# First attention: the join of both sides' weights on GpSimd in place of VectorE, and second copies of turned weights on VectorE in place of ScalarE

## The reference

```python
def block(args):                      # one row block of 128 queries
    i, qb1, qb2 = args
    qpos = i * QB + jnp.arange(QB)
    mask = kpos[None, :] <= qpos[:, None]
    def probs(qb, k):
        s = jnp.einsum('bhqd,bshd->bhqs', qb, k).astype(jnp.float32) * scale
        return jax.nn.softmax(jnp.where(mask, s, -jnp.inf), axis=-1)
    a = probs(qb1, k1) - lam * probs(qb2, k2)
    return jnp.einsum('bhqs,bshe->bhqe', a.astype(v.dtype), v)
```

## Time and profile before

| | |
|---|---|
| three runs | 2420.66, 2422.44, 2423.96 us |
| the profiled execution | 2422.4 us, and its span is 2422.4 us |
| PE busy | 2333.4 us (96% of the span), 12906 matmuls |
| DVE busy | 1497.8 us (62%), 1897 instructions |
| ACT busy | 989.8 us (41%), 1496 instructions |
| POOL busy | 200.9 us (8%), 254 instructions |
| mean granted TensorE clock | 0.996 of full speed |
| the first attention | about 1368 to 1593 us of the span |

### The profile page before, as it was taken

The page is one execution under the profiler, slowest core; times in us unless marked ns, Lnnn a source line. Parts: engine busy times, 40 slices in busy tenths (PEclk is TensorE's granted clock), DMA queues, the critical chain, the costliest instruction groups (busy, mean ns, idle before and its releaser), DMA issues.

```text
span 2422.4 us, 30366 instructions
## 1 busy us (share of the span) xinstructions
PE 2333.4 (96%) x12906; PEld 1249.1 (52%) x12906; DVE 1497.8 (62%) x1897; ACT 989.8 (41%) x1496; POOL 200.9 (8%) x254
## 2 busy tenths in 40 slices
PE   7999999999999999999999977899999999989999
PEld 5445444444444444445544456654444446777765
DVE  6898856644644455588742389865534416989962
ACT  6245344221212121433322488842323216888841
POOL 0001030000000000533301100012000000000000
PEclk9999999999999999999999999999999999999999
DMA  5011000201111102013111010020130200010021
GB/s 184 35 60 45 1 35 36 104 35 70 36 70 35 70 35 70 1 37 116 59 70 35 1 36 1 1 105 35 70 139 29 76 2 1 1 36 1 1 88 53
DMA packets 50487, 116.02 MB, mean 48 GB/s; under 512 B 2418, under 2 KB 8107, under 8 KB 49968
## 3 DMA queue, kind: packets, MB, share of 16 engines
q1 hardware_dynamic: 48616, 105.40, 12.3%
q10 hardware_dynamic: 1736, 8.68, 0.9%
HBM read 101.49 MB, written 12.58 MB: 47 GB/s over the span
## 4 chain that ended last, share of the span: by engine, by line
PE 81%; DVE 10%; ACT 7%; issue 1%; DMA 0%; SPq 0%; DVEq 0%; ACTq 0%
PE PS L72 78%; PE PS L75 4%; ACT RG L81 3%; DVE mx L110 2%; DVE RG L107 2%; DVE R L93 2%; ACT OV L84 2%; DVE R L101 1%; DVE RG L93 1%; DVE RG L101 1%; ACT R L81 1%; DVE oss L110 1%; ACT mx L81 0%; DVE scl L110 0%; DMA R<-in_x 0%
## 5 line engine op out<-in xcount | busy, mean ns | idle before, releaser
L72 PE MATMUL PS<-R,RG 128*128 128x512 f16 (+1 forms) x5472 | 1163.6, 374 | 8.4 <-DVE R L101 4.2
L72 PEld LDWEIGHTS PS<-R,RG 128*128 128x128 f16 (+1 forms) x5472 | 540.4, 103 | 625.8 <-issue 10.5
L72 PE MATMUL PS<-RG,R 128*128 128x512 f16 (+1 forms) x2904 | 631.3, 378 | 2.2 <-DVE R L101 1.7
L72 PEld LDWEIGHTS PS<-RG,R 128*128 128x128 f16 x2904 | 283.4, 98 | 330.5 <-issue 3.0
L81 ACT ACTIVATE R<-PS,scl 128x512 f32<-128x512 f32 (+1 forms) x176 | 116.2, 685 | 646.8 <-PE PS L72 520.8
L101 DVE SCALAR_TENSOR_TENSOR R<-PS,scl,R 128x512 f32<-128x512 f32 (+1 forms) x227 | 161.5, 744 | 184.2 <-PE PS L72 163.5
L101 DVE SCALAR_TENSOR_TENSOR RG<-RG,scl 128x4096 f16<-128x4096 f32 (+2 forms) x52 | 190.6, 3665 | 54.1 <-ACT RG L81 54.1
L107 DVE TENSOR_TENSOR_SCAN RG<-RG 128x127 f32<-128x127 f32 (+7 forms) x128 | 168.4, 1343 | 80.2 <-ACT RG L81 80.0
L72 PE MATMUL PS<-R,OV 128*128 128x64 f32 (+2 forms) x1456 | 195.7, 276 | 5.7 <-DVE R L93 5.4
L110 DVE TENSOR_REDUCE scl<-RG 128x1 f32<-128x4096 f32 (+2 forms) x43 | 155.6, 3619 | 65.3 <-DMA RG<-in_a_w_in 24.7
L81 ACT ACTIVATE RG<-RG,scl 128x4096 f16<-128x4096 f32 (+2 forms) x52 | 158.6, 3050 | 90.2 <-DVE scl L113 90.2
(11 more groups left out here) (128 smaller groups left out, 1522.3 us busy)
## 6 DMA issues: line engine op xcount, KB each, us to landing
RG<-in_w_ff SPq DMA_DIRECT2D x16, 2048.0 KB, 8.2
RG<-in_a_w_in SPq DMA_DIRECT2D x8, 2048.0 KB, 8.6
xspill<-R ACTq DMA_DIRECT2D x2, 4096.0 KB, 16.3
RG<-in_w_kv SPq DMA_DIRECT2D x4, 2048.0 KB, 8.1
RG<-in_b_w_in SPq DMA_DIRECT2D x4, 2048.0 KB, 8.1
RG<-in_w_in SPq DMA_DIRECT2D x3, 2048.0 KB, 8.3
R<-in_x SPq DMA_DIRECT2D x8, 512.0 KB, 8.3
RG<-in_w_out SPq DMA_DIRECT2D x2, 2048.0 KB, 7.9
```

The costliest lines, as they stand in the source:

```text
L72: return self.engine.matmul(*a, **k) if self.engine else Nothing()
```

## The change

VectorE keeps the reciprocal and the ratio and signals `ratio`. GpSimd's new `join(v)` multiplies `e2` by the ratio in place, one `tensor_scalar` a head, and adds all heads of the group to `ea` with one `tensor_tensor`; it signals `joined_a`. The two partition reductions come after groups 30 and 35 of its loop. VectorE's ratio of v waits in addition for `joined_a` of v-2, whose ratio columns it writes over. Part 1 of the copies (`turned_late`) moves from ScalarE to VectorE, behind the ratio of the same iteration; the last one stands between `finish_half` and `finish_low`. The second products wait for `turned_late`.

```diff
--- before.py
+++ after.py
@@ -435,6 +435,9 @@
         def da_scale(u, c, x=0):
 
             return 8 * (u % 4) + c * len(da_groups[u][1]) + x
+
+        def da_ratio(v, j, n):
+            return oss[:, 8 * (v % 2) + 4 * j:8 * (v % 2) + 4 * j + n]
 
         def l_sum(c, i, h, n=1):
             return ls[:, 64 * c + 8 * i + h:64 * c + 8 * i + h + n]
@@ -892,7 +895,7 @@
                         bo = banks.ap(("pva", i, h // 4))
                         for j in range(i + 1):
                             at = width(i) * x + 128 * j
-                            e.wait_ge(*sig("turned_a").at(v, at // 512))
+                            e.wait_ge(*(sig("turned_late").at(v) if at // 512 else sig("turned_a").at(v, 0)))
                             mm = e.matmul(bo[:, 128 * (h % 4):128 * (h % 4) + 128], AT[v % 2][:, at:at + 128],
                                           VV[:, j, 128 * h:128 * h + 128], start=(j == 0), stop=(j == i))
                     mm.then_inc(*full.up("pva", i, hs[-1]))
@@ -1728,6 +1731,17 @@
                 e.wait_ge(*full.at("za", u, sides[-1]))
                 e.tensor_reduce(out, z, AX.X, ALU.max, negate=True).then_inc(*sig("top_a").up(u, sides[-1]))
 
+            def turned_late(v):
+
+                if 0 <= v < N and len(halves(da_width(v))) == 2:
+                    s, at, n = halves(da_width(v))[1]
+                    e.wait_ge(*full.at("ta", v, s))
+                    if v >= 2:
+                        i, hs = da_groups[v - 2]
+                        e.wait_ge(*full.at("pva", i, hs[-1]))
+                    e.tensor_copy(AT[v % 2][:, at:at + n], banks.ap(("ta", v, s))[:, 0:n]).then_inc(
+                        *banks.empty([("ta", v, s)], sig("turned_late"), v))
+
             N = len(da_groups)
             for u in range(N + 4):
                 if u < da_first:
@@ -1738,19 +1752,16 @@
                 if 1 <= u < N + 1:
                     v = u - 1
                     i, hs = da_groups[v]
-                    w, n = width(i), len(hs)
-                    a, a2 = ea(v), e2(v)
-                    ri, ro = oss[:, 8 * (v % 2):8 * (v % 2) + n], oss[:, 8 * (v % 2) + 4:8 * (v % 2) + 4 + n]
+                    n = len(hs)
                     e.wait_ge(*sig("exp").at(v, 1))
-                    e.reciprocal(ri, l_sum(1, i, hs[0], n)).then_inc(*step.up())
+                    if v >= 2:
+                        e.wait_ge(*sig("joined_a").at(v - 2))
+                    e.reciprocal(da_ratio(v, 0, n), l_sum(1, i, hs[0], n)).then_inc(*step.up())
                     e.wait_ge(*step.last())
-                    e.scalar_tensor_tensor(ro, l_sum(0, i, hs[0], n), lamt[:, 5:6], ri, ALU.mult,
-                                           ALU.mult).then_inc(*step.up())
-                    e.wait_ge(*step.last())
-                    for x in range(n):
-                        ax = a[:, w * x:w * x + w]
-                        join = e.scalar_tensor_tensor(ax, a2[:, w * x:w * x + w], ro[:, x:x + 1], ax, ALU.mult, ALU.add)
-                    join.then_inc(*sig("joined_a").up(v))
+                    e.scalar_tensor_tensor(da_ratio(v, 1, n), l_sum(0, i, hs[0], n), lamt[:, 5:6], da_ratio(v, 0, n),
+                                           ALU.mult, ALU.mult).then_inc(*sig("ratio").up(v))
+                if u <= N:
+                    turned_late(u - 2)
                 if 3 <= u < N + 3 and da_groups[u - 3][1][-1] % 4 == 3:
                     i, hs = da_groups[u - 3]
                     g = hs[-1] // 4
@@ -1789,6 +1800,7 @@
                     finish_root(0)
                     for x in range(8):
                         finish_half(x % 4, x // 4)
+                    turned_late(N - 1)
                     for x in range(8):
                         finish_low(x % 4, x // 4)
             finish_mean(1)
@@ -2382,7 +2394,6 @@
                     exp(u, 0)
                 if u == N:
                     finish_root(0)
-                turned(u - 2, 1)
                 if 3 <= u < N + 3 and da_groups[u - 3][1][-1] % 4 == 3:
                     i, hs = da_groups[u - 3]
                     g = hs[-1] // 4
@@ -2649,9 +2660,26 @@
                 e.wait_ge(*sig("o_out").at(i, 1))
                 e.tensor_tensor(o3, o3, r3, ALU.mult).then_inc(*sig("o_gated_pool").up(i))
 
-            measure(31)
-            e.wait_ge(*sig("o_peak").at())
-            across(col(124), col(123)).then_inc(*sig("o_top").up())
+            def join(v):
+                i, hs = da_groups[v]
+                w = width(i)
+                e.wait_ge(*sig("ratio").at(v))
+                e.wait_ge(*sig("exp").at(v, 1))
+                n = len(hs)
+                for x in range(n):
+                    b = e2(v)[:, w * x:w * x + w]
+                    e.tensor_scalar(b, b, da_ratio(v, 1, n)[:, x:x + 1], None, ALU.mult).then_inc(*sig("pool_step").up())
+                e.wait_ge(*sig("pool_step").last())
+                a, b = ea(v)[:, 0:n * w], e2(v)[:, 0:n * w]
+                e.tensor_tensor(a, a, b, ALU.add).then_inc(*sig("joined_a").up(v))
+
+            for v in range(len(da_groups)):
+                join(v)
+                if v == da_first + 8:
+                    measure(31)
+                if v == da_first + 13:
+                    e.wait_ge(*sig("o_peak").at())
+                    across(col(124), col(123)).then_inc(*sig("o_top").up())
             finish_tile(7)
```

## The result

The changed kernel takes 2544.18 us (median of 4 runs, 2538.09 to 2547.79) beside 2421.55 (median of 4) for the kernel before on the same chip. The ratio on record is 1.0495, with a 95% interval of 1.0474 to 1.0516; the two medians alone would give 1.0506. By the medians it is slower by 123 us, where 58 were forecast, and the time lies outside the forecast range.

A forecast was written before the change was run, and what follows sets the result against it. The prediction took waits among TensorE, VectorE and ScalarE as the bound, then a two-group chain through GpSimd's join. Terms 16.3 + 13.8 + 3.1 + 22 + 3 = +58.2 on 2422.4 gave 2480 us, range 2455 to 2503.

The forecast's parts named there:

- the scaling's price: GpSimd's scaling in each join: 0.19 us + 1.05 ns a column, 1.27 us at 1024, at most the addition's cost.
- The chain of two groups with its gates: Widths 384 to 1024: the path through the join spans two groups, 11.12 us at 1024; +16.3 us, output gates +13.8.
- The clock in ordinary rounds: Rival, 11%: TensorE's clock also falls behind ordinary waits for joins, in one pair of three, 15 us more: 2495 us.
- one of the prediction's own signs of being wrong: On TensorE: the forecast is wrong if transposes of 0.6 us take 1.0 in most rounds.
- The two pauses: GpSimd, around the two reductions between joins: some 11 us of each reach TensorE, +22 us, and two clock falls, +3.
- The six narrow groups: Groups of widths 128 and 256: their joins lie beside 10 us of other matmuls and cost 0.
- The end: After the last groups: last join ends 2.5 us later, last copy stands on VectorE before the low halves; +3.1 us.
- The copies: Second copies of turned weights, widths above 512, moved to VectorE: in idle time at large widths, 0 except at the end.
- Outside the stage: Everything outside the first attention: nothing the change touches runs there, so its time is unchanged, 0.
- the join stays hidden: Rival, 3%: in the first attention the join stays off the path and VectorE is relieved, sum -15 us: 2407 us.
- the pauses cost nothing: Rival, 11%: the pauses around GpSimd's two reductions are hidden or absent, so the sum lacks its last two terms: 2455 us.
- VectorE and GpSimd hinder each other: Rival, 7%: in the join's stage additions take 1.55 us, 22% more, and the join terms grow by 14 us: 2494 us.

The follow-up runs named there:

- the cleaned run: Changed kernel without the partition reductions, with extra transposes in TensorE's waits of every second group and the first six groups joined on VectorE: 2483.13 us, ratio 1.0246.
- the filled waits: Changed kernel with 10 or 20 extra TensorE transposes ahead of the wait for the join in even groups from width 384 up: 2522.98 us, ratio 1.0393.
- the six blocks without the reductions: Widths 384 to 1024 of the changed kernel with both partition reductions replaced by one-column copies on GpSimd: 2515.48 us, ratio 1.0367.
- the join of 3.3 us: Changed kernel with the scaling on VectorE behind the ratio, GpSimd only adding; 3.3 us is its join at width 1024: 2479.64 us, ratio 1.0223.
- two groups in the chain: Changed kernel with GpSimd's scaling written as a product with the repeated ratio column, both reductions kept: 2510.64 us, ratio 1.0347.
- with three: Changed kernel with the scaling as that product, both reductions kept, and everything from the transposes on one group later: 2454.00 us, ratio 1.0123.

## Why the prediction was wrong

The direction and the chain that was to decide were right. The step that failed first is a term of the sum, the scaling's price. With its measured length alone the sum would have been about 2509 us (2480.6 + 26.6 + 1.6 at the end), outside the range; the other steps of the list took it to 2544. The difference of 121.1 us between the profiled executions, by the prediction's own steps:

- **The chain of two groups with its gates**, forecast 16.3 + 13.8 = 30.1: the cleaned run, that of the section on whether the parts add up, comes within 1.3 us of it, once the join's length is the measured one. The addition's 2.35 us at 1024 columns was read from a row that is the product with the output gains; that the addition costs the same (2347 ns) was luck.
- **The scaling's price** is the first step that failed: "not above the two-input addition, which does more". That was a reason, not a row. The true slope of 2.50 ns is above the addition's 2.11. A join is longer by 0.65, 0.83, 1.01, 1.20, 1.38 and 1.58 us at the six widths than forecast, 6.65 in all, four pairs a block: **+26.6**. The upper end of the forecast, 2500, rested on this bound.
- **The clock in ordinary rounds** was a rival at 11% and 15 us. It held: 21 us by the filled waits; **+17.5** where no reduction is in the way (the six blocks without the reductions against the cleaned run: 250.6 - 233.1). It was put at one pair in three; outside the two pauses the transposes came slower behind 14 of 22 waits of 1 us and more for a join, at widths from 384 up, which was one of the prediction's own signs of being wrong. It was doubted because the earlier trace rows showed 1.00 beside idle time. Its waits are shorter, up to 1.82 us, but one of those is longer than the 1.71 us of the earlier trace rows, and the transposes behind it took 0.61 us (the lines below this list). So neither nor the earlier trace rows could decide it, and what sets the clock behind a given wait stays open here. It was weighed as independent of the forecast, while a longer join makes it more likely: with the join of 3.3 us the clock was 1.00 at widths 640 and 1024, where the changed kernel had 0.84 and 0.87.
- **The two pauses**, forecast 22 + 3 with the clock: 29.1 by the two blocks without them, +4 on the forecast. The 6.6 and 7.1 us around a reduction are as in the earlier trace rows.
- **The six narrow groups**, forecast 0: **+8.2** (the stage's first maximum to that of width 384, 37.08 us where it was 28.87). With these joins on VectorE the 28.63 us block falls to 19.95. GpSimd still had a product of 1024 columns with the output gains, from 1382.40 to 1384.74, and then pays the fixed 0.29 us a head: 2.35 us for four scalings of 128 columns. The 10 us of matmuls beside them did not cover it; a part of it is clock (0.82 in this stretch, 0.94 before).
- **The end**, forecast +3.1: +6.3 (1686.62 to 1708.55, 21.93 us where it was 15.66). Of the extra 3.2, 1.6 are the longer scaling; the copies alone make the end 2.9 longer.
- **The copies**, forecast 0 outside the end: 7 us when alone, where VectorE also has the join; in the changed kernel not told apart from nothing (1.9 us by the stages of two profiled executions). This fits the cover that was named, the idle time that the leaving join opens.
- **Outside the stage**, forecast 0: the rest is 5.7 us longer, and the stage began 1.9 us earlier. Over all profiled runs the rest lies between 828.0 and 838.4 us with no relation to the change (829.2 before), so this is spread, not effect.

The wait of 1.82 us in the kernel before, and the transposes behind it:

```profile
1457.99 0.99 PE L72 MATMUL PS<-R 64*128 64x512 f16 x12 [1.82 <-ACT RG L81]
...
1459.03 0.61 PE L75 MATMUL PS<-ident,RG 128*128 128x128 f32 x4
```

Sum: 30.1 + 26.6 + 29.1 + 17.5 + 8.2 + 6.3 + 5.7 - 1.9 = 121.6, against 121.1. The agreement is closer than the method: the first two terms are the forecast's own, for eight groups of width 1024, and stand for 56.1 us that the stretches leave over, of which 2.4 lie in blocks 384 to 640 between two kernels that should not differ there.

Of the rivals, "the join stays hidden" and "the pauses cost nothing" fell. "VectorE and GpSimd hinder each other" is true in one direction: VectorE's ratio takes 0.79 us in place of 0.22 at 1650.17 and ends at 1650.96, with GpSimd's addition (1650.94). From width 384 up this is so of all 19 ratios that took over 0.3 us, each ending within 0.02 us of an addition's end. For GpSimd it costs next to nothing, since the next scaling could not start before that addition's end; what VectorE's 9 us in all (48 ratios of 0.41 us in place of 0.22) cost, no run shows. This fits the Trainium skill (SBUF — State Buffer, Who interferes with whom), whose lock holds a VectorE instruction with two SBUF inputs until GpSimd's ends; the additions themselves kept 2.35 us. The rule of the Trainium skill (GPSIMD Engine Reference, Performance versus the Vector engine) for a small one-input body, 1.03 cycles an element, does not fit: 2.50 ns are 3.0 cycles at the 1.2 GHz that it counts in.

## What to carry over

Before moving work to an engine that is idle, find the chain that its result belongs to and how many rounds that chain spans: the same joins and reductions cost 84 us with two groups in the chain and 30 with three, and without the reductions the wide blocks were no longer than before. A bound needs a row, and where the trace has none for an operation, the nearest row of another operation is no end of the range. Waits and TensorE's clock are one risk, not two: here many of the longer waits were paid twice, and more work for TensorE bought time back.

## What was not expected of the hardware

- GpSimd's scaling of a float32 tensor in SBUF by a column or a constant costs 2.50 ns a column (0.61 us at 128, 2.85 at 1024 by a column), the addition of two tensors 2.11 (2.35 at 1024), and the product with one column repeated 1.67 (1.89 at 1024). VectorE takes 0.75 us for the same scaling.
- A partition reduction of 0.38 us between GpSimd's elementwise instructions takes 14.1 us out of its time (6.58 + 0.38 + 7.10). Here that cost 11 to 17 us of the stage each time.
- 400 extra transposes on TensorE made the kernel 21 us faster, by a granted clock of 1.00 in place of 0.84 to 0.95 in four of the six blocks.
